# RMSNorm per subtile inside the FFN and PLE tails, and the next inputs loaded inside the PLE, in a two-layer hybrid decoder trunk

## What is computed

```python
for i in range(2):
    if i == 0:
        h = h + pool_mixer(rmsnorm(h, pool_norm), pool_w, pool_scale)   # causal means over 2, 4, 8, 16 tokens, minus the token
    else:
        k, v = shared_kv(h, ...)                                         # rmsnorm, matmul, k-norm, rotary
        q = rope(rmsnorm((rmsnorm(h, attn_norm) @ w_q), q_norm))
        h = h + sliding_sink_attention(q, k, v, sinks) @ w_o             # window 128, 16 heads of 64, 4 kv heads
    u = rmsnorm(h, ffn_norm[i])
    h = h + (swiglu(u, w_gu, w_down) if i == 0 else moe_swiglu(u, ...))  # dense 2816; 8 experts of 1024, gates of the top 2
    gate = sigmoid(rmsnorm(h, ple_gate_norm[i]) @ ple_gate_w[i])
    h = h + gate * (p[i] @ ple_w[i])                                     # "PLE"
```

## Time and profile before

| | |
|---|---|
| median of 2 runs | 6921.69 us (6795.67 to 7047.71) |
| the profiled execution | 6345.93 us, span of the slowest core 6344.4 us |
| spans of the eight cores | 6275.0 to 6344.4 us |
| PE busy | 4801.5 us, 76% |
| VectorE, ScalarE, GpSimd busy | 2526.2 us (40%), 1555.5 us (25%), 311.9 us (5%) |
| chain that ended last | PE 65%, DMA 13%, DVE 8%, ACT 6% |
| DMA | 143 GB/s on average, 267 to 322 GB/s in the first eighth |

### The profile page before, as it was taken

How to read it: one execution, slowest core, us unless ns; L and a number is a source line. 1 busy time by engine, 2 the same in 40 slices (tenths; PEclk the granted TensorE clock), 3 DMA queues, 4 the chain that set the end, 5 groups by cost and what they waited for, 6 DMA issues and landing times.

```text
span 6344.4 us, 69401 instructions; the slowest of 8 cores (6275.0 to 6344.4 us)
## 1 busy us (share of the span) xinstructions
PE 4801.5 (76%) x23332; PEld 2206.6 (35%) x23332; DVE 2526.2 (40%) x4144; ACT 1555.5 (25%) x2203; POOL 311.9 (5%) x420
## 2 busy tenths in 40 slices
PE   0014448789687987799688987799688987799898
PEld 0001123334343443344333443344333433344343
DVE  1122234454335433444344433444345443454443
ACT  1222132331214211331214211331224211331211
POOL 1111010000001000000001000000001000000000
PEclk9997668899798997899798998899799998899899
DMA  8999952334343434335343434334342334344443
GB/s 267 315 322 320 315 163 82 101 102 144 114 127 100 122 116 128 107 103 152 98 131 96 122 116 128 107 114 141 99 142 86 120 124 133 94 128 128 134 144 121
DMA packets 555722, 904.82 MB, mean 143 GB/s; under 512 B 36336, under 2 KB 463472, under 8 KB 532848
## 3 DMA queue, kind: packets, MB, share of 16 engines
q1 hardware_dynamic: 521088, 801.28, 41.4%
q0 software_dynamic: 34288, 99.10, 4.4%
HBM read 809.61 MB, written 94.90 MB: 143 GB/s over the span
## 4 chain that ended last, share of the span: by engine, by line
PE 65%; DMA 13%; DVE 8%; ACT 6%; issue 5%; POOL 2%; SPq 0%; DVEq 0%; ACTq 0%; POOLq 0%
PE psF L563 17%; PE psF L531 16%; PE psF L536 16%; PE psF L613 4%; DMA sb_QT<-we_gu 3%; DMA sb_QT<-we_down 3%; PE psT L505 3%; PE psF L689 2%; PE psF L753 2%; PE psF L677 2%; ACT sb_uTa L509 2%; DMA sb_ringA<-w_gu 1%; DVE sb_junk L490 1%; PE psF L716 1%; POOL sb_rtt L653 1%
## 5 line engine op out<-in xcount | busy, mean ns | idle before, releaser
L531 PE MATMUL psF<-sb_uTa,sb_ringA 128*128 128x512 bf16 x5504 | 1351.6, 390 | 182.1 <-DMA sb_ringA<-s_gu 147.6
L563 PE MATMUL psF<-sb_ringA,sb_hm 128*128 128x512 bf16 x5504 | 1252.8, 384 | 99.6 <-DMA sb_ringA<-s_down 52.7
L536 PE MATMUL psF<-sb_uTa,sb_ringA 128*128 128x512 bf16 x5504 | 1317.4, 383 | 0.0
L541 DVE SCALAR_TENSOR_TENSOR sb_mm<-sb_th,psF 128x512 f32<-128x512 f32 x688 | 472.1, 686 | 1311.6 <-PE psF L536 1216.5
L540 ACT ACTIVATE sb_th<-psF 128x512 f32<-128x512 f32 x688 | 407.8, 596 | 1964.6 <-PE psF L531 1867.0
L531 PEld LDWEIGHTS psF<-sb_uTa,sb_ringA 128*128 128x128 bf16 x5504 | 533.6, 100 | 856.4 <-issue 282.9
L563 PEld LDWEIGHTS psF<-sb_ringA,sb_hm 128*128 128x128 bf16 x5504 | 528.1, 99 | 757.4 <-issue 179.6
L536 PEld LDWEIGHTS psF<-sb_uTa,sb_ringA 128*128 128x128 bf16 x5504 | 544.3, 99 | 669.6 <-issue 47.8
L573 DVE SCALAR_TENSOR_TENSOR sb_h<-psF,sb_gates,sb_h 128x512 f32<-128x512 f32 x512 | 383.7, 750 | 394.8 <-PE psF L563 389.3
L543 DVE SCALAR_TENSOR_TENSOR sb_hm<-psF,sb_mm 128x512 bf16<-128x512 f32 x688 | 476.1, 692 | 73.9 <-DVE sb_mm L541 2.3
L505 PE MATMUL psT<-sb_ident,sb_u 128*128 128x128 bf16 x1280 | 154.1, 299 | 447.7 <-DVE sb_u L499 328.1
(11 more groups left out here) (147 smaller groups left out, 3171.4 us busy)
## 6 DMA issues: line engine op xcount, KB each, us to landing
sb_ringA<-s_egu SPq DMA_DIRECT2D x256, 1024.0 KB, 10.3
sb_ringA<-s_ed SPq DMA_DIRECT2D x128, 1024.0 KB, 14.1
sb_ringA<-s_gu SPq DMA_DIRECT2D x88, 1024.0 KB, 9.8
sb_ringB<-we_gu SPq DMA_DIRECT2D x96, 512.0 KB, 12.4
sb_ringA<-s_down SPq DMA_DIRECT2D x40, 1024.0 KB, 8.5
sb_ringA<-s_pg SPq DMA_DIRECT2D x32, 1024.0 KB, 6.9
sb_ringA<-w_gu SPq DMA_DIRECT2D x32, 512.0 KB, 14.2
sb_h<-x SPq DMA_DIRECT2D x32, 512.0 KB, 5.8
```

Of the source, the lines that this page charges most:

```text
L531: ins = e.matmul(psF[:, ba, :], lhsT=sv[:, kc, jj, 0:128], rhs=uTa[:, kc, :], start=(kc == 0), stop=(kc == 7))
L536: ins = e.matmul(psF[:, bg, :], lhsT=sv[:, kc, jj, 128:256], rhs=uTa[:, kc, :], start=(kc == 0), stop=(kc == 7))
L541: T.op("dve", lambda e: e.scalar_tensor_tensor(out=mm[tb][:], in0=th[tb][:], scalar=1.0, in1=psF[:, bg, :], op0=ALU.add, op1=ALU.mult), re ...
L563: ins = e.matmul(psF[:, b, :], lhsT=hm[hb][:, jx, s * 128:(s + 1) * 128], rhs=dv[:, q, half * 512:(half + 1) * 512], start=(jx == 0), stop ...
```

## The change

1. RMSNorm is cut into `norm_sub(s)` (sum of squares, mean, Sqrt, reciprocal and `u` of *one* subtile, each with its own dependency record) and `norm_T(s)` (its transpose and copy). `uTa` and `uTb` get a record per subtile. Everywhere one Sqrt on four columns becomes four Sqrts on one column.
2. In the last `down_units` of an FFN, a hook runs `norm_sub(s)` after subtile s, and the transpose of subtile s-1 (`LagNorm.done`). `ple` transposes the last one when it needs it.
3. `ple` runs subtile by subtile, with both halves inside. In layer 1 a hook after each subtile stores it and loads the next tile's x subtile.
4. The pooling stage computes its statistics per subtile, and the FFN's norm of subtile s-1 follows the pooling of subtile s.
5. `p` is loaded ahead of the FFN, and its transposes stand behind the up part of the FFN's first group.
6. The `cost=` numbers of `merge` are changed (8 matmuls 2.2 to 1.75, Sqrt 1.6 to 0.25 plus 1.28 when the table changes), and PE now also waits on its own semaphore for an earlier write to the same PSUM bank.

```diff
         own = self.sem.get(e)
-        if own is not None and sem is own and (not self.same or e == "pe"):
+        if own is not None and sem is own and not self.same:
             return
...
-            norm_stats(hc, Bhc, ss, Bss, rstd, Brstd)
+        def norm_to_uT(hc, Bhc, stream, label="first"):
+            LBL[0] = label
             for s in range(NSUB):
-                ub = ub0 + s % 2
-                make_u(hc, Bhc, s, ub, rstd, Brstd)
-                yield P([Bu[ub]], [BpT[k]])
-                transpose_to(k, u[ub], Bu[ub], 8, uT_[:, :, s * 128:(s + 1) * 128], BuT_)
+                norm_sub(hc, Bhc, s, stream)
+                yield from norm_T(s, stream)
+
+        class LagNorm:
...
+            def done(self, s, keep=1):
+                norm_sub(self.hc, self.Bhc, s, self.stream)
+                self.pending.append(s)
+                yield from self.flush(keep)
...
+                if hook is not None:
+                    yield from hook(s)
...
-            for half in range(2):
-                si = wsA(s_pg[l][:, :, half * 512:(half + 1) * 512], B_s_pg[l])
-                sv = ringA[si][:, 0:8 * 512].rearrange("p (k n) -> p k n", k=8)
-                for s in range(NSUB):
+            sis = [wsA(s_pg[l][:, :, half * 512:(half + 1) * 512], B_s_pg[l]) for half in range(2)]
+            for s in range(NSUB):
+                if lag is not None:
+                    yield from lag.need(s)
+                for half in range(2):
+                    si = sis[half]
...
+                    if half == 1 and tail_hook is not None:
+                        yield from tail_hook(s)
...
+            def finish(s):
+                T.dma("pool", [(out_d[t0 + s * 128:t0 + (s + 1) * 128, :], hc[:, s, :])], reads=[Bhc[s]], sem_on=(Bhc[s], "r"))
+                if next_x is not None:
+                    t1 = next_x * TM
+                    T.dma("sp", [(hc[:, s, :], x_d[t1 + s * 128:t1 + (s + 1) * 128, :])], writes=[Bhc[s]], sem_on=(Bhc[s], "w"))
...
+                    if do_ffn and s >= 1:
+                        yield from lnp.done(s - 1, keep=0)
```

More of the change, by code:

```diff
@@ L136, in op @@
         start = max(self.clock[e], rt + 0.1)
+        if e == "pe" and start > self.clock[e]:
+            self.gaps[self.tag] = self.gaps.get(self.tag, 0.0) + (start - self.clock[e])
         end = start + (self.COST[e] if cost is None else cost)
+        self.busy[e] = self.busy.get(e, 0.0) + (end - start)
         self.clock[e] = end
@@ L901, in build @@
         build.stats = (T.ninst, T.nwait, T.nsem, nc.sbuf_bytes_remaining)
+        build.sim = dict(T.clock)
+        build.busy = dict(T.busy)
+        build.gaps = dict(T.gaps)
     return nc
```

202 lines of the change are left out of this document (150 added, 52 removed).

## The result

The changed kernel takes 0.9737 of the time of the kernel before, 95% interval 0.9667 to 0.9807. That is a gain clear of the noise, but the interval ends just past a gain of 2%, so at a threshold of 2% the verdict is **unclear**. The profiled execution took 6148.85 us where that of before took 6345.93: 197 us less, where the prediction's sum had 176. The medians over all runs are 6226.14 us (12 runs) and 6566.57 us (10 runs, the two shown before the prediction among them).

The account below looks back on a forecast made before the run. PE was taken to bound the periods, its idle time and low clock being what could be had. Savings at places 1 to 3 less losses elsewhere gave 176 us: 6921.7 - 176 = 6745, range 6705 to 6800, out to 6600 and 6890.

Parts of the forecast that it names:

- the four places: PE's idle time, 115 us per period: down part to PLE, PLE to pooling, inside pooling, tile end.
- Places 1 and 2: Last expert's (8 times) and last dense (7 times) down part to PLE end: saved 15.1 and 12.6 us each.
- Place 3: PLE to first pooling matmul, 6 times: 19.5 us idle falls to 5.1 through earlier stores and loads, saved 14.4.
- Place 4: Pooling stage to first FFN matmul, 6 times: 43.0 us grows to 50.5, norms in series, lost 7.5.
- Place 5: Tile end, last PLE matmul to kv projection, 7 times: 23.8 us grows to 31.5, lost 7.7.
- p's transposes: Moved out of the PLE: hidden in the attention, 2.7 us exposed where there is none, 7 times.
- Self-waits: PE's waits on its own semaphore, about 2300: taken as 0; bound 0.1 us each, 230, if none were covered.
- The prediction's bound of 15: First 815 us, conversion of the weights: DMA-bound, same bytes, unchanged within -15 and +15 us.
- The level: Whole time: saving of 176 us taken off the median 6921.69 of the runs shown, 6745; on the profiled 6345.9, 6170.
- rival of longer runs: Whole kernel: denser matmuls bring the longer of the two runs shown, 7047.7 - 176 = 6872; chance 0.06.
- Clock falling in the tails: Rival: PE's gaps of 2.1 to 2.9 us halve its clock, 6.9 per tail, saved only 72, 6850; chance 0.13.
- Table reloads: Rival: 18 extra Sqrts per period each pay two loads, 154 slower, 7075; chance 0.08, shared with chains outweighing the gain.

Follow-up runs that it names:

- e1: Changed kernel with only the tails' part kept: pooling stage, stores and loads, and tile-end norms as in the kernel before; 6140.31 us, ratio 0.971.
- e3: Changed kernel with the hook behind each PLE subtile dropped, stores and loads written after the whole last PLE; 6147.56 us.
- e5: As e3, and each store also waits for the fourth subtile, so the early transfer is gone; 6268.32 us, ratio 0.983.
- e9: Changed kernel with the next subtile's pooling sum, Sqrt and u ahead of this one's copy, and separate u buffers for the FFN norm; 6051.84 us.
- e8: Changed kernel with the transposes of p back at the head of the PLE; 6227.42 us, ratio 0.980.
- e7: Changed kernel without TensorE's waits on its own semaphore; 6172.93 us.
- e12: Changed kernel with a one-column Tanh added behind each Sqrt of the per-subtile norms; 6379.1 us (one execution), 421 table loads.
- e6: Changed kernel with the two tile-end norms also done by subtile inside the dense layer's PLE, one subtile between norm and transpose; 6206.47 us.
- e10: Changed kernel with tile-end norms in the dense PLE, experts' sums taken in the dense FFN, last transposes left to the stages using them; 6260.04 us.

## Why the prediction was right, and where it was wrong

**What bounds it: right.** PE's idle time at the four places was what was to be had; PE is busy 587 of 682.6 us now.

**Places 1 and 2: right.** 39.2 and 37.9 us where 39.6 and 38.5 were worked out, with the gaps in the places named (2.1 expected before the first transpose, 1.83 measured; the third gate behind the Tanh and its table load, 1.09). e1 shows that this is the gain. In sum the eight tails saved 112 and not 121: in four of them the clock falls behind the gap ahead of the down part (40.9 us instead of 39.2), and those of before averaged 54.1, not 54.7.

**Place 3: right in size, and in its cause only by half.** 5.37 where 5.1 was predicted. The prediction tied the early transfer to the hooks; e3 shows that the hook does nothing, and e5 that the transfer is worth 67 of the 84 us. The PLE by subtile makes it early. But the two halves of this place are not to be added: with either of them alone it falls by 3 or 4 us, with both by 14.

**Place 4: right.** 50.57 where 50.5 was predicted. e9 shows the chain: one subtile after another because of program order and shared buffers.

**Place 5: wrong in size.** The failed step is "the last transpose of stream B, whose copy stands behind the router's table load and four Exps... kv projection at 31.5. Lost 7.7." The order was right, the conclusion was not (the section on the change itself says that only the fourth subtile's projection depends on this copy):

```profile
2545.46 0.99 PE L871 MATMUL psF<-sb_wr,sb_uTa 128*128 128x8 bf16 x32 [1.43 <-ACT sb_uTa L537]
2546.31 1.01 PE L533 MATMUL psT<-sb_ident,sb_u 128*128 128x128 bf16 x8
...
2547.11 3.62 PE L768 MATMUL psF<-sb_ringB,sb_uTb 128*128 128x512 bf16 x8
...
2549.49 1.48 ACT L880 ACTIVATE sb_ex<-sb_Lg,sb_nv 128x8 f32<-128x8 f32 x4
...
2550.87 1.00 ACT L537 ACTIVATE sb_uTb<-psT 128x1024 bf16<-128x1024 bf16 x1
```

The last copy does stand behind the Exps, until 2551.87, but nobody waits for it: the change also split the buffer uTb by subtile, and the first kv projection reads only the first (the fourth comes at 2636.63). It starts at 25.1, and all these places together cost 26 us and not 56. Of the 26, 15 stand at the second tile's end alone (26.4 us before, 41.7 after); the six later ones cost 1.4 each on average, and the last experts' norm 2.4. Why the second tile's end is longer was not taken apart; with p's transposes in the PLE (e8) it is 30.4.

**The rest.** p's transposes: +19 predicted; the six later dense parts show +21, but the experts' parts lost 33 more, for which the sum had nothing; with p's transposes away they are 30 shorter (e8), without the self-waits 14 (e7). 24 of the 33 stand in three of the eight parts, 414 us each where before had 405 to 407; without the self-waits two or three of them are still at 413, without p's transposes none is, so most of these 24 go with p. Self-waits: 0 taken, 14 to 33 measured, at about 0.01 us for each of some 2300. Up to the second tile's first FFN matmul the kernel came out 18 us better. The prediction's bound of 15 was for the first 815 us, and it holds: the first tile's last down part starts 6 us earlier. The rest is the first tile's own tail (77.5 us instead of 84.3) and the places behind it, which the sum left out. Left out, too, is the second tile's dense part, 26 us shorter on this core (5 on six of the eight). That the sum of 176 came within 21 us of the profiled 197, and equals the 176 between the medians of the cores, is partly luck: the terms left out and the errors of place 5, of the tails and of the experts' parts cancel.

**The level: wrong, and with it the time.** The failed step is "The runs shown are 450 to 702 longer than it (median 6921.69). I keep the saving in microseconds... 6921.7 - 176 = 6745". The profiled execution at 6345.9 was the one number of the kernel's own level at hand, and it lay 450 us below the lower of two runs that differed by 251 us between them. The sum on it, 6170, is within 0.4% of the profiled 6148.85 and lay outside the range given. What the runs showed in place of the base of 6921.7: a median of 6566.57 us over ten executions of the kernel before, with the shortest at 6320.47, and 6226.14 and 6145.47 for the changed one. The right reading of two such runs and one profile 7% below them was a time near 6170 or near 6745, and a range that holds both. The prediction's rival of longer runs took them to depend on the change; the series show both kernels spread widely (before 6317 to 7091, changed 6145 to 6851).

**The rivals.** Clock falling in the tails: it did in part. In three of the six later dense tails it fell behind the gap of 2.62, as the rival had it, for 0.2 us each, since the rest is under VectorE's chain. In four of the eight experts' tails it fell behind the gap ahead of the down part, for 1.7 us each. The rival's price was 6.9 in each of fifteen. Table reloads: 167 loads against 169. The Trainium skill (ScalarE: Activation LUTs, "Table sets: the hidden batching unit") says to batch activations by table set. The traces agree where Sqrt and Tanh alternate (e12 is 211 us longer, e6 and e10 have 36 and 30 loads more), and they show that a Sqrt per subtile brings no switch as long as only Squares and copies stand between. That a switch is dearer than the load alone, as the prediction has it from the skill, they do not show: the 160 loads of e12 right behind a Sqrt have 2.8 us of idle time before them in all, and a Sqrt starts 0.02 us after its load (2357.27, 1.28 long, then 2358.57).

## What to carry to other kernels

Work by subtile pays where the next stage can start on a part, and it needs a buffer split as finely as the work. Give a hook into a tail a distance of one subtile between making and using (a reading of these traces, not tested alone), and count the table switches that it brings: the next norms put into the PLE's tail gained nothing with that distance (e6) and lost some 110 us without it (e10). A DMA's place in the program decided nothing here, where its queue was empty; what it waits for did, so look at the loop that finishes the data. Two halves of one place can be worth far more together than alone. And when the runs' times and the profiled execution lie 7% apart, predict on both levels.

## What the runs showed of the hardware

A table load of 1.28 us cost 0.8 on the path in e12, although ScalarE is busy only a quarter of the span in the kernel before. Waits of PE on its own semaphore cost about 0.01 us each on average (14 to 33 us for some 2300); most show no idle time, and 59 of them cost 10.4 us in all. Gaps of PE up to 1.83 us inside the experts' tails left the granted clock at 1.00. Behind the same gap of 2.16 us it stayed up in some tails and fell in others, where 32 matmuls took 8.75 us against 7.07, and likewise behind 2.62 us in the dense tails. The seven microseconds with only small transposes in e8 brought the next gates to 3.06 us for eight matmuls against 1.89.
